# Two decoder layers on one core: TensorE's second layer placed inside both expert branches, an earlier slot for one weight chunk, and the last norm shared by two engines

## What is computed

```python
# layer 0: RMSNorm -> projection -> RWKV-7 | gated MLP -> output projection, + x
# layer 1: RMSNorm -> projection -> RG-LRU | dilated attention -> output projection, + x
for l in range(2):
    x = x + mixer[l](rmsnorm(x, norm_mix[l]))
    x = x + hier_moe(rmsnorm(x, norm_ffn[l]), ...)   # 16 experts of 1024 x 512, two per token
y = rmsnorm(x, norm_final)
...
def hier_moe(t):
    hid = silu(t @ w_gate) * (t @ w_up) * gates      # per expert
    return sum_over_experts(hid @ w_down)
```

## Time and profile before

| | |
|---|---|
| median of three runs | 1141.65 us |
| profiled execution, time | 1145.79 us |
| profiled execution, span from first to last instruction | 1144.0 us |
| mean granted TensorE clock | 0.961 |
| PE busy | 1076.3 us (94%) |
| DVE busy | 804.7 us (70%) |
| ACT busy | 640.1 us (56%) |
| moved by DMA | 271.07 MB, mean 237 GB/s |

### The profile page before, as it was taken

The page is one execution under the profiler, slowest core; times in us unless marked ns, Lnnn a source line. Parts: engine busy times, 40 slices in busy tenths (PEclk is TensorE's granted clock), DMA queues, the critical chain, the costliest instruction groups (busy, mean ns, idle before and its releaser), DMA issues.

```text
span 1144.0 us, 17555 instructions
## 1 busy us (share of the span) xinstructions
PE 1076.3 (94%) x7410; PEld 899.2 (79%) x7410; DVE 804.7 (70%) x901; ACT 640.1 (56%) x652; POOL 16.2 (1%) x23
## 2 busy tenths in 40 slices
PE   8999999999999999999967988889999999999996
PEld 8999889877688888888856956568768888888884
DVE  5358545475778989989852676374578898988983
ACT  4556223433666777777742332464367777777672
POOL 0000000000000000000003000000000000000000
PEclk9989999699999999999987989989999999999998
DMA  9332100225479999999926478562458999999961
GB/s 345 122 112 81 39 3 3 75 100 200 185 287 355 351 351 351 361 358 350 359 90 249 148 272 313 204 254 97 162 216 312 353 350 346 361 360 357 357 241 48
DMA packets 40324, 271.07 MB, mean 237 GB/s; under 512 B 5056, under 2 KB 5520, under 8 KB 9520
## 3 DMA queue, kind: packets, MB, share of 16 engines
q1 hardware_dynamic: 39616, 267.11, 63.2%
q0 software_dynamic: 624, 2.76, 0.6%
HBM read 265.78 MB, written 4.07 MB: 236 GB/s over the span
## 4 chain that ended last, share of the span: by engine, by line
PE 84%; DVE 6%; ACT 3%; DMA 3%; issue 3%; SPq 0%; DVEq 0%; ACTq 0%
PE ps L908 10%; PE ps L909 10%; PE ps L910 10%; PE ps L934 5%; PE ps L936 5%; PE ps L935 5%; PE ps L355 4%; PE ps L356 4%; PE ps L357 4%; PE ps L1716 3%; DMA arena<-in_k_near 3%; PE ps L946 1%; PE ps L921 1%; PE ps L947 1%; ACT w_hi L340 1%
## 5 line engine op out<-in xcount | busy, mean ns | idle before, releaser
L347 DVE TENSOR_TENSOR w_lo<-raw,w_hi 128x2048 fp32r<-128x2048 f32 x76 | 174.0, 2289 | 46.8 <-ACT w_hi L340 46.8
L340 ACT ACTIVATE w_hi<-raw 128x2048 fp32r<-128x2048 f32 x76 | 145.4, 1914 | 93.8 <-PE ps L357 38.0
L347 DVE TENSOR_TENSOR lo_more<-raw_more,hi_more 128x2048 fp32r<-128x2048 f32 x48 | 109.9, 2289 | 20.6 <-ACT hi_more L340 20.6
L347 DVE TENSOR_TENSOR w_lo<-raw_more,w_hi 128x2048 fp32r<-128x2048 f32 x48 | 109.9, 2290 | 15.6 <-ACT w_hi L340 15.5
L347 DVE TENSOR_TENSOR lo_more<-raw,hi_more 128x2048 fp32r<-128x2048 f32 x48 | 109.9, 2290 | 15.3 <-ACT hi_more L340 15.3
L340 ACT ACTIVATE hi_more<-raw 128x2048 fp32r<-128x2048 f32 x48 | 91.9, 1915 | 27.6 <-PE ps L910 27.6
L355 PE MATMUL ps<-h_hi,w_hi 128*128 128x320 f32 x320 | 103.2, 323 | 0.0
L340 ACT ACTIVATE w_hi<-raw_more 128x2048 fp32r<-128x2048 f32 x48 | 92.0, 1917 | 16.8 <-PE ps L936 16.8
L356 PE MATMUL ps<-h_lo,w_hi 128*128 128x320 f32 x320 | 101.0, 316 | 0.0
L357 PE MATMUL ps<-h_hi,w_lo 128*128 128x320 f32 x320 | 100.6, 314 | 0.0
L340 ACT ACTIVATE hi_more<-raw_more 128x2048 fp32r<-128x2048 f32 x48 | 91.9, 1914 | 11.4 <-PE ps L936 10.0
(11 more groups left out here) (502 smaller groups left out, 2335.4 us busy)
## 6 DMA issues: line engine op xcount, KB each, us to landing
raw<-in_stream SPq DMA_DIRECT2D x125, 1024.0 KB, 7.0
raw_more<-in_stream SPq DMA_DIRECT2D x96, 1024.0 KB, 7.1
arena<-in_k_near SPq DMA_DIRECT2D x8, 1024.0 KB, 9.5
arena<-in_v_near SPq DMA_DIRECT2D x8, 1024.0 KB, 7.5
arena<-in_k_far SPq DMA_DIRECT2D x8, 512.0 KB, 5.2
arena<-in_v_far SPq DMA_DIRECT2D x8, 512.0 KB, 5.0
arena<-in_bias_prompt SPq DMA_DIRECT2D x1, 1536.0 KB, 7.7
xt<-in_x SPq DMA_DIRECT2D x2, 640.0 KB, 4.8
```

Of the source, the lines that this page charges most:

```text
L340: eng.activation(hi_slot(W_SLOT[c]), raw_chunk(c), ACT.Copy).then_inc(S("w_hi_made"), 1)
L347: eng.tensor_tensor(lo_slot(W_SLOT[c]), raw_chunk(c), hi_slot(W_SLOT[c]), ALU.subtract).then_inc(S("w_lo_made"), 1)
```

## The change

There are five edits. PE's second layer is passed to `moe_pe` of layer 0 as a function and is emitted at the end of both the sorted and the dense branch, so it is in the program twice and PE reaches it without leaving the branch. `W_LAST[AT_IN1]` names a chunk four earlier: the last expert's second gate chunk and not its second up chunk. In layer 0's sorted way, four unread matmuls of 512 columns stand ahead of the last turn and six ahead of the last down product, and `warm(30)` becomes `warm(12)`. The root's table load moves from the head of `final_act` to a place ahead of the last `y_keep` of layer 1. And the last norm is rearranged: DVE multiplies each block by `norm_final` as soon as it is squared, reading PSUM and writing `y_rows`; then DVE scales the first halves and ACT the second halves by the reciprocal root; SP waits for both.

```diff
-W_LAST = [AT_IN1 - 3 if c == AT_IN1 else last_in_slot(W_SLOT, c) for c in range(STREAM)]
+W_LAST = [AT_IN1 - 7 if c == AT_IN1 else last_in_slot(W_SLOT, c) for c in range(STREAM)]
...
-        def moe_pe(eng, layer, at):
+        def moe_pe(eng, layer, at, rest=lambda: None):
...
             with eng.If(read_flag(eng, layer)):
                 sorted_pe(eng, layer, at)
+                rest()
             with eng.Else():
                 dense_pe(eng, layer, at)
+                rest()
...
+            def keep_busy(n):
+
+                eng.wait_ge(S("silu_made"), HT * (e0 + NE))
+                for _ in range(n):
+                    eng.matmul(ps[:, GATE_BANK, :], x_hi[0][:, 0:P], x_hi[0], start=True, stop=True)
...
             if layer == 0:
+                keep_busy(4)
                 turn(NE - 1)
+                keep_busy(6)
                 down(at + MOE_CHUNKS - 2, NE - 1)
...
             hid_split(NE - 1)
+            if layer:
+                eng.activation(small[:, 327:328], eps_norm, ACT.Sqrt)
             y_keep(3, 0)
...
+        sq_left = [overlay(f"sq_left{n}", 6144 - LOW + 512 * n, [P, 512], F32)[:, :] for n in range(6)]
+
+        def final_rows(n):
+
+            a, b = TOKEN_TILES[n % 3]
+            return b - a, ps[0:b - a, FINAL_BANK[n % 3][n // 3], :], y_rows[0:b - a, n % 3, 512 * (n // 3):512 * (n // 3) + 512]
+
         def final_act(eng):
-            eng.activation(small[:, 327:328], eps_norm, ACT.Sqrt)
+
+            def root(i):
+                m = final_rows(i)[0]
+                eng.wait_ge(S("rms_base"), 3)
+                eng.wait_ge(S("squared"), 16 + i)
+                eng.activation(rms_root[0:m, i:i + 1], sums_sq[0:m, 1, i:i + 1], ACT.Sqrt, bias=rms_base[0:m, i:i + 1], scale=1.0 / D)\
+                   .then_inc(S("rms_root"), 1)
+
             for n in range(6):
-                a, b = TOKEN_TILES[n % 3]
+                m, row, _ = final_rows(n)
                 eng.wait_ge(S("rows_done"), n + 1)
...
+                eng.activation(sq_left[n][0:m, :], row, ACT.Square, accum_out=sums_sq[0:m, n // 3, n % 3:n % 3 + 1]).then_inc(S("squared"), 1)
+            for i in range(3):
+                root(i)
+            for i in range(3):
+                m, _, out = final_rows(3 + i)
+                eng.wait_ge(S("final_weighted"), 4 + i)
+                eng.wait_ge(S("final_rstd"), i + 1)
+                eng.activation(out, out, ACT.Identity, bias=zero[0:m, :], scale=rstd_tok[0:m, i, :]).then_inc(S("y_second"), 1)
 
         def final_dve(eng):
...
             eng.wait_ge(S("final_w_loaded"), 16)
-            for i, (a, b) in enumerate(TOKEN_TILES):
+            for n in range(6):
+                m, row, out = final_rows(n)
+                eng.wait_ge(S("squared"), 13 + n)
+                eng.tensor_tensor(out, row, final_w[0:m, 512 * (n // 3):512 * (n // 3) + 512], ALU.mult).then_inc(S("final_weighted"), 1)
+                if n == 2:
+                    eng.tensor_scalar(rms_base, sums_sq[:, 0, :], 1.0 / D, 1e-6, ALU.mult, ALU.add).then_inc(S("rms_base"), 1)
+            for i in range(3):
+                m, _, out = final_rows(i)
                 eng.wait_ge(S("rms_root"), 7 + i)
...
+                eng.reciprocal(rstd_tok[0:m, i, :], rms_root[0:m, i:i + 1]).then_inc(S("final_rstd"), 1)
+                eng.wait_ge(S("final_rstd"), i + 1)
+                eng.wait_ge(S("final_weighted"), i + 1)
+                eng.tensor_scalar(out, out, rstd_tok[0:m, i, :], None, ALU.mult).then_inc(S("y_scaled"), 1)
...
-            warm(30)
+            warm(12)
...
-                eng.wait_ge(S("y_scaled"), 2 * i + 2)
+                eng.wait_ge(S("y_scaled"), i + 1)
+                eng.wait_ge(S("y_second"), i + 1)
                 eng.dma_start(outs["y"][0:b - a, i, :], y_rows[0:b - a, i, :]).then_inc(S("y_stored"), 16)
...
             mix0_pe(eng)
-            moe_pe(eng, 0, AT_MOE0)
-            mix1_pe(eng)
-            moe_pe(eng, 1, AT_MOE1)
+
+            def second_layer():
+                mix1_pe(eng)
+                moe_pe(eng, 1, AT_MOE1)
+
+            moe_pe(eng, 0, AT_MOE0, second_layer)
```

More of the change, by code:

```diff
@@ L1167, in final_act @@
             for n in range(6):
-                a, b = TOKEN_TILES[n % 3]
+                m, row, _ = final_rows(n)
                 eng.wait_ge(S("rows_done"), n + 1)
-                eng.activation(y_rows[0:b - a, n % 3, 512 * (n // 3):512 * (n // 3) + 512], ps[0:b - a, FINAL_BANK[n % 3][n // 3], :], ACT.Square,
-                               accum_out=sums_sq[0:b - a, n // 3, n % 3:n % 3 + 1]).then_inc(S("squared"), 1)
-            eng.wait_ge(S("rms_base"), 3)
-            for i, (a, b) in enumerate(TOKEN_TILES):
-                eng.wait_ge(S("squared"), 16 + i)
-                eng.activation(rms_root[0:b - a, i:i + 1], sums_sq[0:b - a, 1, i:i + 1], ACT.Sqrt, bias=rms_base[0:b - a, i:i + 1], scale=1.0 / D)\
-                   .then_inc(S("rms_root"), 1)
+                eng.activation(sq_left[n][0:m, :], row, ACT.Square, accum_out=sums_sq[0:m, n // 3, n % 3:n % 3 + 1]).then_inc(S("squared"), 1)
@@ L1178, in final_dve @@
+            for i in range(3):
[5 more added lines that the diff above has]
+                eng.activation(out, out, ACT.Identity, bias=zero[0:m, :], scale=rstd_tok[0:m, i, :]).then_inc(S("y_second"), 1)
         def final_dve(eng):
-            eng.wait_ge(S("squared"), 15)
-            eng.tensor_scalar(rms_base, sums_sq[:, 0, :], 1.0 / D, 1e-6, ALU.mult, ALU.add).then_inc(S("rms_base"), 1)
@@ L1181, in final_dve @@
             eng.wait_ge(S("final_w_loaded"), 16)
-            for i, (a, b) in enumerate(TOKEN_TILES):
-                eng.wait_ge(S("rms_root"), 7 + i)
[L1184 to L1188, removed]
+            for n in range(6):
[4 more added lines that the diff above has]
+                    eng.tensor_scalar(rms_base, sums_sq[:, 0, :], 1.0 / D, 1e-6, ALU.mult, ALU.add).then_inc(S("rms_base"), 1)
```

## The result

| | before | changed |
|---|---|---|
| median of five runs | 1141.34 us (1134.95 to 1144.91) | 1125.88 us (1119.09 to 1130.94) |
| ratio, 95% interval | | 0.9861, 0.9826 to 0.9896 |
| profiled execution, its time / span | 1145.79 / 1144.0 us | 1119.09 / 1117.2 us |
| mean granted clock | 0.961 | 0.985 |

The change is faster by 15.9 us (0.0139 of 1141.34), with an interval of 11.9 to 19.9. The forecast was 24.0.

What follows compares the result with a forecast made beforehand. TensorE was nearly always busy, so time lay in its idle or half-clock stretches, chiefly the passage from layer 0 to layer 1: 21.3 us (3.4, 2.8, 9.2, 6.0, rounded) plus 2.7 at the end, 24.0, gives 1117.7 us; range 1112 to 1125.

Steps and rivals of the forecast that it cites:

- The slot wait: Layer 0's last expert: ACT and DVE split `AT_IN1` without waiting for PE, so the hidden product starts 3.4 us earlier.
- The clock: Layer 0's last turn and down product run at full clock because PE idles less: 2.8 us gained.
- The branch: Join after layer 0's scatter: with the code inlined, PE's waits of 6.3 and 2.9 us go, 9.2 us.
- the unread matmuls: Layer 1's start: twelve at full clock take 1.8 us where thirty took 7.75, gaining 6.0 us.
- Does layer 1 keep it? ... I charge nothing: Layer 1: transfers stay in time, the tightest chunk with 3 us to spare, so no loss was charged.
- The end: Last norm: table load off the path and scaling shared by DVE and ACT gain 2.7 us, bounds 1.5 to 3.2.
- the slow end: Whole kernel: no clock gain and the short gain in the last norm leave 16 us, 1125.5 us.
- late code in the straight program: Rival: PE's code arrives late even without a jump, costing 2.9 or 6.3 us, 1120.6 to 1124; chance 0.12.
- half clock at the turn: Rival: the clock drops all the same at the turn or in the scatter, 3.9 us lost, 1121.6; chance 0.06.
- two branches at the end: Rival: PE's two exits from branches take 6.3 us each and set the end, 3.7 later, 1121.4; chance 0.07.
- a longer program that is loaded late at every block: Rival: every block of the doubled program loads late, costing 2.92 us each, so slower at 1191; chance 0.04.
- The transfers take it back: Rival: PE waits on in layer 1, which inherits only the 6.2 us SP gains, plus 2.7, 1132.8; chance 0.02.

Runs made afterwards that it cites:

- no_keep: Changed kernel without the four and six unread matmuls around layer 0's last turn; 1124.18 us, 0.9858 of the kernel before.
- slot_only: Kernel before with only the `W_LAST[AT_IN1]` wait moved four chunks earlier; 1135.2 us, 0.9958.
- inline_only: Kernel before with only PE's second layer emitted inside both branches, thirty unread matmuls and old slot wait kept; 1134.02 us, 0.9946.
- act_end_inside: Changed kernel with ACT's `final_act` moved inside both branches of layer 1's experts; 1122.99 us, 0.9835 of the kernel before.
- root_at_head: Changed kernel with the root's table load put back at the head of `final_act`, outside the branch; 1129.04 us, 0.989 of the kernel before.
- old_end_inside: Changed kernel with the earlier last norm (DVE alone scales), inside the branches, table loaded ahead of the last `y_keep`; 1126.54 us, 0.9859 of the kernel before.
- no_pool_adds: Changed kernel without POOL's nine additions of the count biases, so attention lacks them; 1121.23 us, 0.9824 of the kernel before.
- counts_early: Changed kernel with the two count arrays loaded ahead of the first keys and values; 1120.87 us, 0.9836 of the kernel before.
- both_mended: Changed kernel with count arrays loaded ahead of the first keys and ACT's last part inside the branches; 1120.85 us, 0.9819 of the kernel before.

## Why the forecast was right in part and too large

**The slot wait (3.4): right.** The turn's distance from the up product fell from 5.44 to 2.06. The 0.8 us of DVE behind PE is there as "issue" ahead of line 1162.

**The clock (2.8): nearly right.** Passage up to the end of the scatter: 5.8 us shorter where 6.2 were forecast (3.4 and 2.8), so 2.4 for the clock. The ten kept-busy matmuls carry 1.6 of it, by no_keep; 0.8 come with the shorter wait alone, by slot_only. In no_keep the waits of PE around the turn alone brought the clock to 0.89, so the 1.00 that I had read off one stretch with waits did not carry over to this one.

**The branch (9.2) and the unread matmuls (6.0): right.** From the scatter's end to the first tile 15.1 us less, forecast 15.2; inline_only shows the branch was both gaps: there this stretch falls from 17.0 to 4.5, by 12.5, of which 3.3 are the thirty matmuls at full clock and 9.2 the gaps. The Trainium skill (Runtime: NRT & Kernel Launch, "Instruction fetch mechanics") says that the sequencer fetches the next page of the program while it executes the current one, and the changed trace agrees, without a wait of PE there. The 51 ns that the prediction took from the Trainium skill (Advanced Engine Details and Errata, "Control Flow Timing") stand there for a branch that is always taken; for a compare-and-branch, which line 531's rows are, it has about 108 ns. The rows, 6.3 and 3.4 us, are far above either. The exit at the end is one branch and not the two that I charged, hidden as before:

```profile
L531 PEldq COMPARE_BRANCH  x1: 3709/3709/3709, 1105.3 to 1105.3; - x1
```

**"Does layer 1 keep it? ... I charge nothing": this step failed.** I asked only whether a transfer would be late. None was. What changed was which work of DVE meets which work of POOL: one went with PE, the other with SP's transfers, and DVE gained 16 us on POOL. Five versions have PE's gap at 4.6 to 5.5 us (changed, act_end_inside, root_at_head, no_keep, old_end_inside): layer 1 takes 519.4 to 523.2, mean 521.2. Three have none or little of it (no_pool_adds none, counts_early 1.6, both_mended 1.1): 515.5 to 516.9, mean 516.3; before, 515.2. So it costs about 5 us. Near the cause it is more: at the 65th matmul of line 357 in layer 1, PE is 39.8 us behind its first tile before, 39.9 in no_pool_adds and 47.1 in the changed kernel, 7.3 for the gap and the half clock behind it. At the last such matmul, the projection's end, no_keep (gap 5.4, mean granted clock 0.94 over the projection) is at 146.5 and the kernel before (0.94 too) at 142.1: 4.4 are left. Where the rest comes back I did not trace. My trace of before had the row that warns: POOL's additions beside a DVE that was idle. No time for them stands anywhere in the prediction's sum.

**The end (2.7): this step failed too.** I took a moved table load for a hidden one. Two loads of 1.28 us replaced one, and ate the gain. Without them 1.7 us are there, within the forecast's bounds of 1.5 to 3.2 but 1.0 under its 2.7. The arrangement on two engines gave 0.7 less than forecast: it has the last rows ready 1.1 us sooner and not 1.8 (the three scalings of ACT take 2.22 us together where I had about 0.6 each). The stores took 0.9 where I took off 0.5, and the load gave 1.5 where I had 1.4.

**The sum.** 20.95 for the passage, less 5.9 for layer 1 (521.16 against 515.24; in the changed kernel's own trace 4.2), and nothing for the end: 15.0 to 16.8, and the runs say 15.9. The range ended at 1125, and its own sum for the slow end was 1125.5, because that end charged for the clock and for a shorter gain at the end, and nothing at all for layer 1. So 1125.88 lies just outside a range that was widened for losses which did not come; the gain itself was 8 us off the forecast. Of the rivals, late code in the straight program, half clock at the turn, two branches at the end and a longer program that is loaded late at every block are all absent from the trace. "The transfers take it back" had the right place, the handing over to layer 1, but a chunk for PE as the thing that doesn't move along, where it was POOL's work.

## What to carry to other kernels

When an edit moves one engine against another, list what each of the other engines does in the stretch it moves into, and look above all for DVE and POOL work that was apart and now meets; a transfer that is in time is not enough. A table load that was moved into a branch was made again behind the join here, so move what uses the table with it, and look in the trace for the loads that are left. A jump over a long branch cost 6.3 us at once and 2.9 nine matmuls later, and what stands straight behind paid neither. Where a kernel's executions spread by half a per cent, cut the profiles at common instructions: a us in a short stretch is visible there that the medians can't show. Layer 1's 515 us are too long for that: the clock moves them by several us.

## What the hardware showed that I had not expected

DVE instructions on four columns took 0.92 to 0.98 us, that is one POOL addition of 384 columns (7.80 us for eight, 0.975 each), and 2.27 beside the one of 1024 (2.34): the wait is for the whole of POOL's instruction in progress, whatever DVE's own size. (The one of 0.72 came 0.3 us into an addition.) It hit `TENSOR_SCALAR` and `TENSOR_TENSOR` with all operands in SBUF. `RECIPROCAL` (0.18) and the operations that read PSUM (line 2444, 0.89 for two, as without POOL) ran through it. POOL in turn was held up: 11.23 us for its eight against 7.80 where DVE was idle, since two of them met a DVE subtraction of 2048 columns that had begun and took 2.38 and 3.08 us. The Trainium skill (SBUF — State Buffer, "SBUF: two separate sides") says that DVE and GpSimd share a pair of ports which whoever starts first holds for a whole instruction, and that this concerns DVE's operations with two SBUF inputs or in a 2-port mode; these rows agree for the operations with two inputs in SBUF and for those that read PSUM; that the `TENSOR_SCALAR` ones were in a 2-port mode no row shows.

The granted clock alone moved a fixed stretch of work, the opening, between 568.8 and 580.4 us over thirteen profiled executions, 2% of it and three quarters of the change's whole gain. Its mean over the opening was 0.99 at 568.8, 0.98 in the five executions at 571.7 to 571.9, and 0.96 in the two at 580.4.
